# Up-projection: every second pair of chunks takes its 256-column matmuls first and its 512-column ones second

## The reference, cut to what matters

```python
h2 = rmsnorm_2(x, norm2_g[l])
u = causal_dwconv(jnp.einsum('bsd,df->bsf', h2, w_up[l]), conv_w[l], conv_b[l])
u_gate, u_val = u[..., :D_FF], u[..., D_FF:]
x = x + jnp.einsum('bsf,fd->bsd', jax.nn.silu(u_gate) * u_val, w_down[l])
```

## Time and profile before

| | |
|---|---|
| three runs, median (lowest to highest) | 2078.66 us (2078.59 to 2079.37) |
| the profiled execution's own time | 2078.61 us |
| its span | 2076.6 us |
| PE busy | 2069.6 us (100% of the span) |
| DVE busy | 1639.4 us (79%) |
| ACT busy | 1159.9 us (56%) |
| matmuls of the up-projection | 704 with `w_hi` into `xs` and as many into `g`, the same numbers with `w_lo` |

### The profile page before, as it was taken

One profiled execution on the slowest core, in us unless ns is written; L12 is line 12 of the kernel. 1 busy time (PEld: TensorE's weight loads), 2 busy tenths in 40 slices (PEclk: granted clock), 3 DMA queues, 4 the chain that ended last, 5 costly groups with the idle time before them and its releaser, 6 DMA issues.

```text
span 2076.6 us, 25506 instructions
## 1 busy us (share of the span) xinstructions
PE 2069.6 (100%) x9916; PEld 1735.0 (84%) x9916; DVE 1639.4 (79%) x1846; ACT 1159.9 (56%) x1387; POOL 50.2 (2%) x53
## 2 busy tenths in 40 slices
PE   9999999999999999999999999999999999999999
PEld 8888888888888887878888888888888888888887
DVE  7988888887888876876788668867777777789986
ACT  6766555555556555555555455555555555555553
POOL 0000000000000000110000000000000000000000
PEclk9999999999999999999999999999999999999999
DMA  8656777677774766655465556455555555556653
GB/s 340 212 198 218 222 234 226 210 245 218 249 262 150 227 205 212 205 151 193 137 229 181 204 182 216 158 179 188 183 193 193 183 198 188 182 191 235 222 203 134
DMA packets 117720, 423.30 MB, mean 204 GB/s; under 512 B 13152, under 2 KB 13920, under 8 KB 117344
## 3 DMA queue, kind: packets, MB, share of 16 engines
q1 hardware_dynamic: 109440, 394.66, 55.2%
q0 software_dynamic: 5184, 18.88, 5.1%
q10 hardware_dynamic: 2976, 8.14, 1.1%
HBM read 419.52 MB, written 2.10 MB: 203 GB/s over the span
## 4 chain that ended last, share of the span: by engine, by line
PE 95%; DVE 3%; ACT 1%; issue 0%; DMA 0%; ACTq 0%; DVEq 0%
PE g L898 49%; PE xs L921 9%; PE xs L768 8%; PE g L768 8%; PE g L925 6%; PE g L739 4%; PE xs L774 4%; PE g L774 4%; DVE w_lo L1773 1%; PE xs L809 1%; ACT w_hi L1290 1%; PE xs L960 1%; PE xs L1093 0%; DMA xf<-in_x 0%; PE xs L1107 0%
## 5 line engine op out<-in xcount | busy, mean ns | idle before, releaser
L1773 DVE TENSOR_TENSOR w_lo<-raw,w_hi 128x1024 fp32r<-128x1024 f32 x631 | 765.6, 1222 | 313.5 <-ACT w_hi L1290 304.9
L1290 ACT ACTIVATE w_hi<-raw 128x1024 fp32r<-128x1024 f32 x631 | 661.7, 1057 | 541.1 <-PE g L898 238.7
L898 PE MATMUL g<-w_hi,in_both 128*128 128x512 f32 x1120 | 356.4, 390 | 1.3 <-DVE w_lo L1848 0.9
L898 PE MATMUL g<-w_hi,mid_both 128*128 128x512 f32 x992 | 320.1, 393 | 0.0
L898 PEld LDWEIGHTS g<-w_hi,in_both 128*128 128x128 f32 x1120 | 210.2, 188 | 46.1 <-issue 1.1
L898 PEld LDWEIGHTS g<-w_hi,mid_both 128*128 128x128 f32 x992 | 186.3, 188 | 38.4
L898 PE MATMUL g<-w_lo,in_both 128*128 128x512 f32 x560 | 217.9, 389 | 0.0
L898 PE MATMUL g<-w_lo,mid_both 128*128 128x512 f32 x496 | 193.1, 389 | 0.0
L768 PE MATMUL g<-mlp_both,w_hi 128*128 128x512 f32 x704 | 169.2, 391 | 0.0
L768 PE MATMUL xs<-mlp_both,w_hi 128*128 128x512 f32 x704 | 167.9, 391 | 0.0
L768 PEld LDWEIGHTS xs<-mlp_both,w_hi 128*128 128x128 f32 x704 | 129.4, 188 | 25.0
(11 more groups left out here) (503 smaller groups left out, 3337.1 us busy)
## 6 DMA issues: line engine op xcount, KB each, us to landing
raw<-in_stream SPq DMA_DIRECT2D x631, 512.0 KB, 4.2
d_block<-in_stream SPq DMA_DIRECT2D x28, 512.0 KB, 4.5
o_block<-in_stream SPq DMA_DIRECT2D x24, 512.0 KB, 4.6
v_block<-in_stream SPq DMA_DIRECT2D x20, 512.0 KB, 4.1
ge_block<-in_stream POOLq DMA_DIRECT2D x15, 512.0 KB, 5.6
gm_block<-in_stream SPq DMA_DIRECT2D x12, 512.0 KB, 5.4
ge_block<-in_stream SPq DMA_DIRECT2D x10, 512.0 KB, 4.6
gl_block<-in_stream POOLq DMA_DIRECT2D x6, 512.0 KB, 5.4
```

What stands on the lines that cost most here:

```text
L898: ins = mm(GG[:, bank, :], a[:, kt, t * P:(t + 1) * P], w[:, slot, half_chunk(j)], start=n == 0 and opens(item, bank), stop=ended and n == ...
L1290: activation(w_hi[:, n % RING, :], of[:], ACT.Copy).then_inc(hi_ready, 1)
L1773: v.tensor_tensor(w_lo[:, n % RING, :], of, w_hi[:, n % RING, :].bitcast(F32), ALU.subtract).then_inc(lo_ready, 1)
```

## The change

From the second group on, in every second pair of a group (chunks 2 and 3, and chunks 6 and 7) the 16 lows now come ahead of the 16 highs. Each half of the pair waits for its own chunk as before: lows for `lo_ready`, highs for `hi_ready`. The count `mm_done` of a chunk goes with the last matmul that uses it, which in such a pair is its last high. The number of matmuls, their sizes and the sums are the same.

```diff
--- before.py
+++ after.py
@@ -763,10 +763,10 @@
                         high_block(b, j, buf, slot, k)
                     return low_blocks(blocks, buf, slot, k, last)
 
-                def high_block(b, j, buf, slot, k):
+                def high_block(b, j, buf, slot, k, last=False):
                     kt = k * ROWS_PER_CHUNK + j
-                    mm(UP[buf][:, b, :, :], w_hi[:, slot, j * COLS + b * P:j * COLS + (b + 1) * P],
-                       a_both[:, :, kt, :], start=(kt == 0), stop=False, skip_group_check=True)
+                    return mm(UP[buf][:, b, :, :], w_hi[:, slot, j * COLS + b * P:j * COLS + (b + 1) * P],
+                       a_both[:, :, kt, :], start=(kt == 0), stop=last and j == ROWS_PER_CHUNK - 1, skip_group_check=True)
 
                 def low_blocks(blocks, buf, slot, k, last):
                     for b, j in blocks:
@@ -784,13 +784,21 @@
                     blocks = [(b, j) for b in range(4) for j in range(ROWS_PER_CHUNK)]
                     if k == 0:
                         pe.wait_ge(group_read[buf], read - 1)
+                    low_first = k // 2 % 2 == 1
+                    if low_first:
+                        for i in range(2):
+                            pe.wait_ge(lo_ready, c + i + 1)
+                            low_blocks(blocks, buf, (c + i) % RING, k + i, False)
                     for i in range(2):
                         pe.wait_ge(hi_ready, c + i + 1)
                         for b, j in blocks:
-                            high_block(b, j, buf, (c + i) % RING, k + i)
-                    for i in range(2):
-                        pe.wait_ge(lo_ready, c + i + 1)
-                        low_blocks(blocks, buf, (c + i) % RING, k + i, k + i == n - 1).then_inc(mm_done, 1)
+                            ins = high_block(b, j, buf, (c + i) % RING, k + i, low_first and k + i == n - 1)
+                        if low_first:
+                            ins.then_inc(mm_done, 1)
+                    if not low_first:
+                        for i in range(2):
+                            pe.wait_ge(lo_ready, c + i + 1)
+                            low_blocks(blocks, buf, (c + i) % RING, k + i, False).then_inc(mm_done, 1)
                 return chunk, two_chunks
 
             def one(phase, g, k, chunk):
```

## The result

The changed kernel takes 2087.64 us (median of 6 runs, 2087.50 to 2087.75) against 2078.70 us before (6 runs, 2078.59 to 2079.37): 1.0043 times as long, with a 95% interval of 1.0032 to 1.0053. The prediction was 2087.2. The profiled execution has a span of 2085.7 us against 2076.6.

A forecast was written before the change was run, and what follows sets the result against it. TensorE, busy throughout the up-projection's 468 us, was taken as the bound. From 2078.6 us, plus 9.4 for ten gate-group stalls, minus 0.8 for fewer switches, came 2087.2 us, 0.41% slower; range 2084.5 to 2090.5.

The forecast's parts named there:

- the stall: Last pair of ten up-projection gate groups: TensorE waits for chunk 7's `w_lo`, 0.94 us each, 9.4 us in all.
- the chain: Gate groups, ACT and DVE: chunk 4's `w_hi` and `w_lo`, `scaled`, `conv_start`, chunk 6's conversions, `conv_taps`, chunk 7's `w_lo` at 1460.57.
- Lateness: Gate groups' last pair: chunk 7's `w_lo` ready at 1460.57, wanted at 1459.79, so 0.78 us late.
- the 0.16: Each stall's cost beyond lateness, 0.05 + 0.11 us, read from one down-projection wait; bounds 0 and 0.27.
- The value groups: 11 up-projection groups: no stall, chunk 7's `w_lo` ready near 1481.68, some 0.4 us ahead of need.
- the earlier place: Value groups: lows first frees chunk 2's place, so ACT's `w_hi` of chunk 6 starts 0.86 us sooner.
- the prediction's rival: Value groups stall as well: 11 waits of 0.62 us, 6.8 us more, 2094.0 us; chance 0.07.
- The switches: TensorE going from lows to highs in up-projection pairs: 42 fewer at 0.02 us, saving 0.8 us (0.4 to 1.3).
- No stall: Gate groups' `conv_start` or `conv_taps` come 0.94 us sooner, so no lows wait: 2077.8 us; chance 0.08.
- slower long runs of lows: Up-projection lows beyond the sixteenth in a row slow from 0.12 to 0.154 us: 23 us more, 2110; chance 0.02.
- that rival: TensorE's clock falls to 1.2 GHz for the pair after each stall, up to 5.57 us each: 2143 us; chance 0.02.

## Why the prediction was right

- **Where the stall is and what it hangs on.** Ten waits, gate groups only, between the two low blocks of the last pair: as forecast. That lateness is the cause is shown from both ends, by moving `conv_taps` behind chunk 7's `w_lo` and by moving the chain's head (no stall either way), and by lengthening the chain (a longer stall). That it is not the order as such is shown by the value groups alone and by chunks 2 and 3 alone.
- **Its size.** Forecast 0.94 us, measured 0.97 by the rows above, and 0.96 as the mean of the ten: the stage is 476.39 - 466.78 = 9.6 us longer than with the same order and no stall. Lateness is 1461.73 - 1460.91 = 0.82 us (0.78 forecast), what comes on top 0.05 + 0.10 = 0.15 (0.16 forecast). That these agree so closely is partly luck: the 0.16 came from one wait of another stage with other matmuls, and its own bounds were 0 and 0.27. The 0.10 lies in the first of the eight lows, recorded as 0.388 us where the others take 0.28, and the record of its weight load starts at 1461.77, with it. That fits the prediction's guess of a load that no matmul covers; no run tests it. The lateness grew by about 0.03 us because TensorE comes to the last pair sooner, 1458.04 + 16 x 0.12 - 1443.30 = 16.66 us behind the group's start instead of 16.70, while the chain ends as late as before, 18.43 us behind it. Ten stalls: 9.6 us by the stage, 9.4 forecast.
- **The value groups.** Room of 0.96 - 0.59 = 0.37 us, some 0.4 forecast (its last step, 1481.68, is 1477.00 + 3.41 + 1.22 = 1481.63 by the spacing in the earlier trace rows, which changes nothing). The run with the last pair alone shows that without the earlier place they would have stalled 11 times. Each of those is 0.63 us, against 0.62 in the prediction's rival.
- **The switches.** Forecast 0.8 us for 42. The two versions without stalls both show 0.82 us less up-projection, and the versions with half of the new order half of that. That is 0.02 us each, as read from the earlier trace rows. The prediction's own bounds of 0.4 to 1.3 were wide, so that hitting 0.8 is in part luck.
- **The rivals.** No stall, stalling value groups and slower long runs of lows did not happen: 32 lows are recorded as 4.00 us, (4.00 - 0.28) / 31 = 0.12 us apart. The clock did not fall in the changed kernel: its ten stalls of 0.97 us left it at 1.00. But the reason for giving that rival two in a hundred was weaker than it looked. It rested on one wait of 0.86 us, and stalls of 2.2 us brought the clock down in eight of ten. By the Trainium skill ("TensorE: Matmul & The Clock Gate", Part 1, The HAM clock gate) an idle engine's clock is halved; the trace of the lengthened chain agrees, with 0.82 in eight pairs. But the page ties the half clock to a spell of idleness and not to every wait, so that the prediction read too much into it when it took 2143 from it for stalls this short: the ten of the change kept 1.00. Between the two lie only the single waits near the start, of 1.57 and 1.75 us as recorded (the lengthened stalls are recorded as 1.96), behind which the clock stayed at 1.00.
- **What stays small.** The profiled executions differ by 2087.67 - 2078.61 = 9.06 us, the up-projection by 8.79. The other 0.3 lies ahead of it. The program is the same up to there, and over all the profiles the up-projection's second group starts anywhere from 1375.3 to 1376.6; the first wait of the program for `w_lo` varies from none recorded to 1.8 us.

## What to carry to other kernels

Before changing the order in which a saturated engine takes its operands, write down for each operand when it is ready and when it will be wanted. An operand that was 2.9 us early is late once its use moves up by 3.65 us, and the few places where its producer is held up by other work (here a block of eight instructions on DVE) are the ones to look at. If the order is worth having, move that other work first: with `scaled` taken early, the same order costs nothing and shortens the stage by 0.8 us, though this is 0.04% of the kernel and inside the interval of its measurement.

## What the runs showed that I had not expected

- Stalls are not additive: 2.2 us in place of 0.97 cost 3.8 us instead of 2.2 in eight of ten cases, since the granted clock fell to 1.2 GHz for part of the pair behind them. The remaining two, with the same recorded wait of 1.96 us, kept 2.4 GHz, and so did single waits of 1.57 and 1.75 us elsewhere.
- A place in the ring that comes free 0.9 us sooner spares eleven groups a stall of 0.63 us, with no other edit: half of the change alone was slower (2094.81 us) than all of it (2087.64).
